# A two-block transformer kernel: gate products in plain fp32, sixteen more tokens by gathered rows

## What is computed

```python
q = (xb @ wq).reshape(PEER_BLOCK, PEER_HEADS, 2, PEER_HALF)
s = jnp.einsum('thpd,hpkd->thpk', q, sub_keys)
s_top, i_top = lax.top_k(s, PEER_TOPK)            # 16 of 128 keys, for both halves
best_s, best_pos = lax.top_k(cand_s, PEER_TOPK)   # 16 of the 16x16 sums, per head
g = jax.nn.softmax(best_s, axis=-1)
act = jax.nn.gelu(jnp.einsum('thkd,td->thk', expert_u[experts], xb))
return jnp.einsum('thk,thkd->td', g * act, expert_v[experts])
```

## Time and profile before

| | before |
|---|---|
| median of 3 runs | 2395.32 us (2394.99 to 2395.55) |
| profiled execution, its own time | 2394.86 us |
| its span, first to last instruction | 2393.0 us |
| TensorE busy (matmul) | 2359.3 us, 99% |
| VectorE, ScalarE, GpSimd busy | 65%, 39%, 52% |
| mean granted TensorE clock | 0.998 |

### The profile page before, as it was taken

One profiled execution on the slowest core, in us unless ns is written; L12 is line 12 of the kernel. 1 busy time (PEld: TensorE's weight loads), 2 busy tenths in 40 slices (PEclk: granted clock), 3 DMA queues, 4 the chain that ended last, 5 costly groups with the idle time before them and its releaser, 6 DMA issues.

```text
span 2393.0 us, 35812 instructions
## 1 busy us (share of the span) xinstructions
PE 2359.3 (99%) x12844; PEld 2121.5 (89%) x12844; DVE 1559.5 (65%) x2832; ACT 944.9 (39%) x1487; POOL 1249.3 (52%) x705
## 2 busy tenths in 40 slices
PE   7999999999999999999999999999999999999998
PEld 4878888899999999999999999998778888888886
DVE  5258435789999999679999999992365225322201
ACT  4374333344555555333333334442353223222312
POOL 3305443447899999455555555444304444444443
PEclk9999999999999999999999999999999999999999
DMA  7237422338978998999999999943202222222221
GB/s 285 80 115 264 180 93 93 132 117 280 319 240 305 321 326 306 393 379 414 413 416 411 417 406 405 376 162 114 75 23 97 97 97 88 97 96 96 96 98 71
DMA packets 179614, 526.15 MB, mean 220 GB/s; under 512 B 18240, under 2 KB 70896, under 8 KB 178224
## 3 DMA queue, kind: packets, MB, share of 16 engines
q1 hardware_dynamic: 120928, 345.24, 39.7%
q0 software_dynamic: 43024, 159.14, 17.2%
q10 hardware_dynamic: 15552, 20.36, 2.4%
HBM read 474.93 MB, written 49.73 MB: 219 GB/s over the span
## 4 chain that ended last, share of the span: by engine, by line
PE 94%; DVE 2%; DMA 2%; POOL 1%; ACT 1%; issue 0%; SPq 0%; ACTq 0%; DVEq 0%
PE bank L1394 22%; PE bank L1396 22%; PE bank L1395 22%; PE pair L1395 6%; PE pair L1394 6%; PE pair L1396 6%; PE pair L1756 2%; DMA wraw<-in_w 1%; PE bank L1924 1%; PE pair L1535 1%; PE bank L1561 1%; PE bank L1574 1%; POOL wlo L720 1%; PE pair L1697 1%; PE bank L1915 0%; PE bank L1907 0%
## 5 line engine op out<-in xcount | busy, mean ns | idle before, releaser
L720 POOL TENSOR_TENSOR wlo<-wraw,whi 128x1024 fp32r<-128x1024 f32 x303 | 741.4, 2450 | 743.6 <-ACT whi L867 742.3
L1394 PE MATMUL bank<-HH,whi 128*128 128x512 f32 (+1 forms) x2048 | 739.3, 361 | 4.8 <-ACT T L1139 2.1
L1396 PE MATMUL bank<-HH,wlo 128*128 128x512 f32 (+1 forms) x2048 | 735.9, 359 | 0.0
L1395 PE MATMUL bank<-HL,whi 128*128 128x512 f32 (+1 forms) x2048 | 735.8, 359 | 0.0
L867 ACT ACTIVATE whi<-wraw 128x1024 fp32r<-128x1024 f32 x456 | 481.8, 1058 | 617.0 <-PE pair L1396 308.0
L1394 PEld LDWEIGHTS bank<-HH,whi 128*128 128x128 f32 x2048 | 385.1, 188 | 47.5 <-issue 7.2
L1396 PEld LDWEIGHTS bank<-HH,wlo 128*128 128x128 f32 x2048 | 384.7, 188 | 40.2
L1395 PEld LDWEIGHTS bank<-HL,whi 128*128 128x128 f32 x2048 | 385.2, 188 | 39.3 <-issue 0.2
L793 POOL DMA_INDIRECT VROW<-in_w,which x128 | 204.6, 1599 | 191.5 <-DVE YROW L2568 178.7
L2500 DVE TENSOR_TENSOR wlo<-wraw,whi 128x1024 fp32r<-128x1024 f32 x153 | 186.3, 1218 | 20.5 <-ACT whi L867 18.7
L786 POOL DMA_INDIRECT X<-in_u_rows,which x128 | 149.9, 1171 | 60.4 <-DVE dots L2342 34.3
(11 more groups left out here) (444 smaller groups left out, 3826.2 us busy)
## 6 DMA issues: line engine op xcount, KB each, us to landing
wraw<-in_w SPq DMA_DIRECT2D x456, 512.0 KB
gate_dram<-GS SPq DMA_DIRECT2D x24, 1024.0 KB
GJ<-gate_dram SPq DMA_DIRECT2D x32, 768.0 KB
act_dram<-actb ACTq DMA_DIRECT2D x108, 184.0 KB
AJ<-act_dram SPq DMA_DIRECT2D x108, 184.0 KB
adaw<-in_ada SPq DMA_DIRECT2D x32, 512.0 KB
ada<-in_ada SPq DMA_DIRECT2D x16, 512.0 KB, 14.8
NB<-in_nab POOLq DMA_DIRECT2D x4, 1024.0 KB
```

The lines of the kernel that those rows point to most:

```text
L720: nc.gpsimd.tensor_tensor(wlo[:, slot, :, :].rearrange("p k c -> p (k c)"), wraw[:, slot, :, :].rearrange("p k c -> p (k c)"), whi[:, slot ...
L1394: pe.matmul(out_, ah, bh, start=first, stop=False, **kw)
L1395: pe.matmul(out_, ah, bl, start=False, stop=False, **kw)
L1396: return pe.matmul(out_, al, bh, start=False, stop=last, **kw)
```

## The change

It is one edit of the table of constants and what follows from it, in seven parts:
1. `FT` is 32 instead of 16. The dense products have 352 columns instead of 368, there are 88 steps instead of 92, and 160 dots and row additions instead of 144; in the V stage a row of the extra tokens comes after every third tile up to tile 95 instead of after every seventh.
2. The gate matmul is plain fp32 with 128 columns, one per token, four to a step in one PSUM bank. There are no high and low halves of the gates; OG has 512 columns instead of 1024.
3. ScalarE copies the four gate matrices of a step out of PSUM at once (`gate_out`); VectorE's addition (`gate_sum`) is gone.
4. ScalarE makes OJ (four activations of 128 columns, iota times -1 plus a column of JTS); GpSimd's `offsets_j` is gone.
5. 92 dots are spread over the 88 steps (46 over 92 before); the tail has 32 (38 before), the V stage 8 (32 before).
6. GpSimd's fetches in the gate stage follow its steps two behind, and it makes all low halves up to tile 102, as before.
7. The last gate group stands after three of eight blocks of tile 100 instead of behind it.

```diff
-FT = 16
+FT = 32
...
-U_POOL = 4 * GATE_IT + GATE_TILES + 3
+U_TAIL = 4 * GATE_IT + GATE_TILES + 3
+U_POOL = 103
...
-GATE_DOT = 2
-PSUM_DOTS = TOP_DOTS + STEPS // GATE_DOT
-U_DOTS = 112
+GATE_DOTS = 92
+PSUM_DOTS = TOP_DOTS + GATE_DOTS
+TAIL_DOTS = 32
+U_DOTS = PSUM_DOTS + TAIL_DOTS
...
-V_DOT_TILES = [10 * m // 3 + 1 for m in range(32)][:DOTS - U_DOTS]
+V_DOT_TILES = [8 * m + 1 for m in range(DOTS - U_DOTS)]
...
-                if q >= 2 * GATE_DOT and q % GATE_DOT == 0:
+                while fetched < R + TOP_DOTS + gate_dots(max(q - 2, 0)):
                     fetch_u(fetched)
...
+            def gate_out(q):
+
+                act.wait_ge(g_done, q + 1)
...
+                nc.scalar.activation(GS[:, q // 16 % 2, :, t:t + 4], bank[4 + q % 3].rearrange("p (t j) -> p j t", t=4), ACT.Copy)\
+                    .then_inc(g_evac, 1)
...
+            def offsets_j(q):
+
+                if q >= 4:
+                    act.wait_ge(og_ready, q - 3)
+                for t in range(4):
+                    ins = nc.scalar.activation(OJ[:, q % 4, t, :], iota[:, :], ACT.Identity, scale=-1.0,
+                                               bias=JTS[:, 4 * q + t:4 * q + t + 1])
+                ins.then_inc(oj_ready, 1)
...
+            for q in range(3):
+                offsets_j(q)
             for n in range(STEPS + 2):
...
+                if n + 3 < STEPS:
+                    offsets_j(n + 3)
+                if n >= 2:
+                    gate_out(n - 2)
...
                 pe.wait_ge(og_ready, q + 1)
-                for h in (2 * q, 2 * q + 1):
-                    if h >= 3:
-                        pe.wait_ge(g_evac, h - 2)
-                    for t in range(2):
-                        e = 2 * (h % 2) + t
-                        mm = pe.matmul(bank[4 + h % 3][:, t * 256:t * 256 + 256], OI[:, 4 * (q % 2) + e, :],
-                                       OG[:, q % 2, :, e, :], start=True, stop=True)
-                    mm.then_inc(g_done, 1)
+                if q >= 3:
+                    pe.wait_ge(g_evac, q - 2)
+                for e in range(4):
+                    mm = pe.matmul(bank[4 + q % 3][:, e * P:(e + 1) * P], OI[:, 4 * (q % 2) + e, :], OG[:, q % 2, e, :],
+                                   start=True, stop=True)
+                mm.then_inc(g_done, 1)
...
-            u_tile(gu0 + GATE_TILES, 0)
+            u_blocks(gu0 + GATE_TILES, 0, range(3))
             gate_group(STEPS - 1)
+            u_blocks(gu0 + GATE_TILES, 0, range(3, KB))
```

More of the change, by code:

```diff
@@ L243, in build @@
         a2 = allocator(s2)
-        OI = a2("OI", [P, 8, P], FR)
-        OG = a2("OG", [P, 2, 2, 4, P], FR)
+        OI = a2("OI", [P, 8, P])
+        OG = a2("OG", [P, 2, 4, P])
         s2.close()
@@ L454, in build @@
         g_done = sem("g_done")
-        g_high = sem("g_high")
         g_evac = sem("g_evac")
@@ L523, in units, with gate_dots @@
             return min(8 * GATE_TILES * n // STEPS, 8 * GATE_TILES)
+        def gate_dots(q):
+            return GATE_DOTS * q // STEPS
         def dot_column(m):
@@ L827, in _ @@
                 lo(G0["U"] + t, t % R)
-            for k in range(fetched, U_DOTS + R):
+                while fetched < R + PSUM_DOTS + (t - U_TAIL + 1) * TAIL_DOTS // (P - U_TAIL):
+                    fetch_u(fetched)
+                    fetched += 1
+            u_fetches = min(U_DOTS + R, DOTS)
+            for k in range(fetched, u_fetches):
                 fetch_u(k)
@@ L1106, in _ @@
                 act_tile(m, u, 16 * (m // 2))
[L1108 to L1115, removed]
+            def gate_out(q):
+                act.wait_ge(g_done, q + 1)
+                if q % 16 == 0 and q >= 32:
+                    act.wait_ge(g_out[q // 16 % 2], 64 * (q // 32))
+                t = 4 * (q % 16)
+                nc.scalar.activation(GS[:, q // 16 % 2, :, t:t + 4], bank[4 + q % 3].rearrange("p (t j) -> p j t", t=4), ACT.Copy)\
+                    .then_inc(g_evac, 1)
             def gate_tile(u):
@@ L1120, in gate_tile @@
                 act_tile(m, u % 4, 16 * (m // 2))
+            def offsets_j(q):
[5 more added lines that the diff above has]
+                ins.then_inc(oj_ready, 1)
             ahead(G0["U"], 4 * GATE_IT)
+            act.wait_ge(j_rows, 1)
+            for q in range(3):
+                offsets_j(q)
             for n in range(STEPS + 2):
-                for h in range(2 * n - 4, 2 * n - 2):
-                    if h >= 0:
-                        gate_high(h, 64 * (h // 64) if h % 32 == 0 and h >= 64 else None)
+                if n + 3 < STEPS:
+                    offsets_j(n + 3)
+                if n >= 2:
+                    gate_out(n - 2)
                 for u in range(units(n) // 8, units(n + 1) // 8):
@@ L2443, in _ @@
             nc.vector.tensor_copy(ITS[:, 0:SD], bank[4][:, 0:SD])
-            then(nc.vector.tensor_copy(GHT[:, :], bank[6][:, 0:SD]))
-            nc.vector.tensor_tensor(GLT[:, :], bank[6][:, 0:SD], GHT[:, :].bitcast(F32), ALU.subtract).then_inc(gt_split, 1)
+            nc.vector.tensor_copy(GT[:, :], bank[6][:, 0:SD]).then_inc(gt_split, 1)
             v.wait_ge(gt_split, 1)
@@ L2453, in window @@
                 nc.vector.tensor_copy(gate_window[:, 0:m], ITS[:, i * P:i * P + m])
[L2454 to L2457, removed]
+                then(nc.vector.tensor_copy(gate_window[:, P:P + m], GT[:, i * P:i * P + m]))
             def indices_hot(q):
                 if q >= 2:
-                    v.wait_ge(g_done, 2 * q - 2)
+                    v.wait_ge(g_done, q - 1)
                 n, ring = q % 32, slice(4 * (q % 2), 4 * (q % 2) + 4)
@@ L2470, in gates_hot @@
                 v.wait_ge(oj_ready, q + 1)
-                oj = OJ[:, q % 4, :, :].rearrange("p t j -> p (t j)")
-                nc.vector.scalar_tensor_tensor(OG[:, q % 2, :, :, :].rearrange("p w t j -> p w (t j)"), bc(oj, 1, 2), 0.0,
-                                               bc(gate_window[:, P + 8 * n:P + 8 * n + 8], 2, P), ALU.is_equal, ALU.mult)\
+                nc.vector.scalar_tensor_tensor(OG[:, q % 2, :, :], OJ[:, q % 4, :, :], 0.0,
+                                               bc(gate_window[:, P + 4 * n:P + 4 * n + 4], 2, P), ALU.is_equal, ALU.mult)\
                     .then_inc(og_ready, 1)
[L2476 to L2482, removed]
             for q in range(STEPS):
@@ L2487, in _ @@
                 indices_hot(q)
-                if q >= 2:
-                    gate_sum(2 * q - 4)
-                    gate_sum(2 * q - 3)
                 gates_hot(q)
-                if q % GATE_DOT == GATE_DOT - 1:
+                while dotted[0] < TOP_DOTS + gate_dots(q + 1):
                     dot()
-            for h in range(2 * STEPS - 4, 2 * STEPS):
-                gate_sum(h)
             def lo(g, slot):
@@ L2512, in expert_weights @@
                 v.wait_ge(w_known, i + 1)
+            v.wait_ge(g_done, STEPS)
             then(nc.vector.memset(kept0[:, :, SD:TD * P], 0.0))
[L2515 to L2519, removed]
+            for t in range(U_TAIL, P):
+                if t == U_POOL:
+                    v.wait_ge(w_lo, G0["U"] + U_POOL)
+                if t >= U_POOL:
+                    lo(G0["U"] + t, t % R)
+                while dotted[0] < PSUM_DOTS + (t - U_TAIL + 1) * TAIL_DOTS // (P - U_TAIL):
                     dot()
```

16 lines of the change are left out of this document (4 added, 12 removed).

## The result

The changed kernel takes 2435.14 us (median of 4 runs, 2431.35 to 2436.08); the kernel before, 2395.15 (4 runs, 2393.35 to 2395.55). The ratio is 1.0166, 95% interval 1.0154 to 1.0178: 1.7% slower, where 2394.3 and a range of 2386 to 2404 were forecast. The loss of 40 us is far outside this.

The account below looks back on a forecast made before the run. TensorE, busy 99%, was taken as the bound: its matmuls plus its waits. Lead +0.7, gate stage +19.8, tail -4.0 and V stage -17.5 sum to -1.0: 2394.9 becomes 2393.9, median 2394.3 us; range 2386 to 2404.

Parts of the forecast that it names:

- V stage: 128 tiles: 499.0 us forecast, -17.5 from 516.5, with 8 us of transfer loss taken as absorbed and 3 as lost.
- gate stage: 60 tiles with 91 of 92 gate groups: 308.3 us plus 1.5 for late transfers, +19.8 from 290.0.
- The step that failed: Gate stage: VectorE waits at dots, maybe about 4 us late before TensorE sees it; 1.5 us put on this.
- The rival with the right sign: Gate stage or V stage: transfers come late and TensorE waits for them; 2403 or 2402 us; together chance 0.23.
- that stall: Tail: TensorE's present stall at a weight load, with its half clock, kept at 4 us.
- ScalarE as the bound: Gate steps: an offset costing 0.40 us gives ScalarE 3.5 us a step plus waits; 2403 us; chance 0.06.
- Lead: U tiles 0 to 39: 5.3 of 6.2 us saved become idle time before the transposes; +0.7 us.
- Half clock: After TensorE's idle time of about 5 us ahead of the transposes, a slowed clock costing 1.7 us.
- Tail: 28 tiles with the last gate group: 112.4 us forecast, -4.0 from 116.4, present stall kept.
- the rival in which the rings absorb everything: V stage -20.5 without transfer loss, tail without half its stall -6.0; whole kernel -7.5, 2387.8 us; chance 0.33.

Follow-up runs that it names:

- the first experiment: Changed kernel with GpSimd's gate-stage gathers asked for ahead of the low half and two steps earlier; 2384.09 us, ratio 0.9956 to the kernel before.

## Why the prediction was wrong, point by point

**What held.** Dense products stand 0.160 us apart, and the eight records of a gate group fit the 0.895 us taken from the earlier trace rows: without waits the gate stage is 308.0 us in five kernels, where 308.3 was worked out. Four offsets take 1.28 us, 1.17 expected. TensorE does wait at the transposes, though 2.9 us and not 5.3.

**The step that failed** is in the gate stage: "VectorE will wait at dots. It may be about 4 us late before TensorE sees it", and the 1.5 us put on it. The stage took 356.3 us, not 309.8: the waits cost 356.3 - 308.3 = 48.0 us where 1.5 were put, so this one term is short by 46.5 us, and the whole prediction by 40.8. I added two margins, two steps from issue to use and 4 us of cover, and compared them with a gather of 9.4 us. Both margins are measured from TensorE's clock. But GpSimd issues a gather behind a low half; that waits for ScalarE's high half, that for `offsets_j(n + 3)` ahead of it in ScalarE's program, and that for OG of step n - 1, which stands behind the dot in VectorE's. So a dot that is late makes the next gather late by as much; the cover is spent once and never refilled. I had every link on paper, "GpSimd fetches four dots ahead and, since its low halves wait for ScalarE, which waits for the tile", but I had ScalarE wait for TensorE's tile alone. In the changed kernel it also waits for VectorE. That wait came with part 4 of the change, and I had priced the part only by its 1.17 us of work. It does harm only together with part 5: with the same wait and 46 dots the stage takes 308.0 us. And it is not the only way round: with the wait moved by one step 26 of the 48 us went, and 22 stayed, with a chain by way of TensorE's own wait for OG. No run keeps the 92 dots and gives the offsets back to GpSimd.

**The rival with the right sign** had another mechanism. It said that TensorE's waits would name the weights and that it decides from about 12 us between issue and landing. The gathers were quicker than that. The profile of the kernel after has no landing times for them, but the gathers in its chain take 5.4 to 9.6 us. Those of the experiments have them, here of the gate stage with the ring open (the first experiment) and with the index three steps behind:
```profile
DMA to landing us min/median/max: 4.0/7.2/10.1
```
```profile
DMA to landing us min/median/max: 4.7/6.0/10.2
```
They land no later where the step is longest, and TensorE's waits name OG. The Trainium skill, "DMA: Bandwidth & Descriptors", section "Queues, rings and completion order", was set beside that rival; in the gate stage the waits do not follow what was drawn from it, and with the ring open the engines carry 352 GB/s without TensorE waiting for weights. In the tail one weight load took 20.4 us in the chain, against 18.2 in the earlier trace rows, as I had assumed by keeping that stall.

**ScalarE as the bound** did not happen by its busy time: 235.6 of 308 us with the ring open, 2.7 us a step, which with its 0.3 of waiting for its own tile are the 3.0 worked out.

**Lead**: forecast +0.7, measured -3.2. VectorE finished at 662.25, not 664.5: one late product took 0.75 us, not the 1.17 of the earlier trace rows, and the rest came sooner. Half clock, which I expected behind the wait, did not come in this kernel; in the first experiment it did, and its lead is 1.5 us longer (160.3).

**Tail**: forecast -4.0, measured +0.9; the stall and its half clock stayed and grew (the clock stood at half for 6.8 us behind it, where it was 3.4 before).

**V stage**: forecast -17.5, measured -20.1, next to the -20.5 of the rival in which the rings absorb everything. I had 1.67 MB a tile for tiles 0 to 63; measured are 246.4 us at 411 GB/s, 101.3 MB or 1.58 MB a tile. The dots' gathers were put at twice their number: of the eight in these tiles four rows were gathered before the stage begins, four slots ahead (the trace has 4 gathers of X there, not 8), and rows are 82, not 85. So 1.58 MB in 3.85 us is just what the engines, which read full (share 1.03), carry: there was hardly a shortage to absorb, and the nearness of the two numbers is no evidence for the rings.

## What to carry to other kernels

When a change adds a wait, follow it round: from the waiting instruction through what stands behind it on its engine, until you are at TensorE or back where you began. If you are back, the slacks of the links do not add up against TensorE's pace; the step is the ring's time divided by the steps that the program leaves for it, and here one step in one index was worth 2, 46 or 96 us, depending on which. Busy shares do not show such a ring; waits of three engines that follow one another round do, and here asking for the transfer a step or two earlier opened it at no cost. Look for a second way round before you trust the quotient: shortening one way left the other here.

## What the hardware showed that I had not expected

A VectorE product of two operands in SBUF (128 x 512) took 11.01 us beside five GpSimd products in a row, 0.69 to 0.75 when none ran, and the 1.17 of the earlier trace rows fits too: in the kernel before a low half ran until 663.92, 0.6 us into it. The Trainium skill, "SBUF — State Buffer", section "SBUF: two separate sides", says that the two engines share a pair of ports as an exclusive lock, that a VectorE operation with two SBUF inputs takes it against a GpSimd operation that reads SBUF, and that whoever comes second is blocked for the other's whole instruction. The traces agree on the blocking; in the one trace with a queue of such operations it lasted through the rest of the first and four more, not through one.

After nearly the same wait of TensorE, 2.9 us, the clock stayed full in the kernel after and fell to half in the first experiment. The windows behind the transposes, first of the kernel after:
```profile
662.50:666.00 3.50, 3.50 (x26) 3.50 (x26) 2.38 (x6) 0.00 (x0) 3.50 (x2) 1.00 0.97 368
```
and of the first experiment:
```profile
663.50:667.00 3.50, 3.50 (x17) 3.50 (x16) 1.63 (x5) 0.00 (x0) 3.50 (x2) 0.56 1.00 378
```
It is worth 1.6 us and divides the kernels with 352 columns and 28 early dots into leads of 158.7 and 160.3; what decides it was not tried.
